# Router, slot gates and the way out of a branch in a two-block float32 kernel

## The chip, the cores and the metric

The kernel runs on one core of a Trainium2 chip. The metric is the device time of one execution in microseconds (us), the median of three runs; lower is better. Each run is compared with the kernel before on the same chip.

## The reference

The input is one sequence of 256 tokens of width 1024 in float32. A first block of two attention layers (dilated windows, grouped queries, attention to a memory) is followed by a second block of two layers. The change lies in the second block, whose layer is, in short:

```python
h = x @ w_in[l]                       # 1892 columns: queries, keys, values, latents
mix = [window_attention(h), sparse_attention_top64(h), latent_attention(h)]
x = layer_norm(ALPHA * x + concat(mix) @ w_out[l], ln1_g[l], ln1_b[l])
scores = sigmoid(x @ w_router)        # 16 experts in 4 groups
group  = argmax(sum of the two best biased scores in each group)
gates  = the two best experts of the group, normalised
y = sum_e gates[e] * (silu(x @ w_gate[l, e]) * (x @ w_up[l, e])) @ w_down[l, e]
x = layer_norm(ALPHA * x + y, ln2_g[l], ln2_b[l])
```

## The kernel before

The 256 tokens are two tiles of 128 rows. Every engine has its own program, written out by hand, and they meet at semaphores. `wait_ge` waits for a point of another engine, `then_inc(*x.did(...))` marks one, and `follow()` makes an engine wait for its own last instruction.

Each float32 weight goes through a ring in memory (filled by SP's DMA queue) and is cut in quarters of at most 128 x 1024: ACT writes the high part (`wH`, line 441), DVE the rest (`wL`, line 449). Five quarters fit (`NQ`). TensorE then makes three single-pass matmuls for one product (`mm3`, lines 508 to 510), and the last of a quarter gives the quarter's place back (`w_used`). A float32 matmul that isn't split appears as two matmul records, a transposition as one.

Stages of a layer `l` of the second block, in order:

- **h{l}0 to h{l}3**, the projections by `w_in`. The first is made tile by tile in `pe_proj_by_tiles`: tile 0, and after its sixth of eight steps the function `second_tile`, which turns tile 1 (8 transpositions, line 1661) and makes the "shift product" (line 1745: eight float32 matmuls of the layer norm's bias with the router's weights, 16 columns each). ACT copies that product (line 1854) and then goes on cutting weights.
- **attention**, in units. `dve_run` lets DVE choose the 64 best keys of a row in rounds of eight (`best`, lines 1991 and 1992) between the softmaxes of the units. Each unit ends with its output Y (line 894 or 1712), which TensorE turns (line 976).
- **p{l}**, the output projection, and layer norm 1: sums (1625), mean (1626), middle (1632), squares on ACT (1652), root by ACT (712, 713) and DVE (718 to 722), the scaled row (1643). Each tile has its own root.
- **router**: TensorE turns each tile's `middle` (1661), runs four multiplications by zero (`pe_idle`, line 517), and multiplies with the router's weights (1829). DVE makes logits (2072), scores and the chosen group (2075 to 2090); TensorE counts ranks (1837); DVE copies them (2095), takes the largest count (2096, 2097) and the slots (2098, 2101).
- **a branch** on the largest count. Here all engines take `few`: tokens are gathered by matmuls (2307), slot gates are made (2314) after the first expert's gate and up product, 16 experts run, and the result goes back (2356).
- **layer norm 2** (`act_finish`, `dve_finish`), still inside the branch; for layer 0 it ends with the turned tile 0 for h10 (`act_flip_exit`, `dve_flip_exit`). Tile 1 is turned after the branch.

The multiplications by zero give nothing to the result. They are placed where TensorE would wait.

Of the kernel before, what the change touches and what calls it, by code (L numbers as in the profile page):

```python
# [125 lines left out]
def program(nc, t, out, cols, keep):  # L126
# [76 lines left out]
    zeroR = sb("zeroR", P, 1, dt=F32R)  # L203
    blank = sb("blank", P, 1)
# [180 lines left out]
    first_normed, first_turned, second_normed = sem("first_normed"), sem("first_turned"), sem("second_normed")  # L385
# [15 lines left out]
    def write(pe, act, dve, pool, sp, branch):  # L401
# [1207 lines left out]
        for l in range(2):  # L1609
            for n, (a, b) in enumerate(SPLITS):  # L1610
                to_heads(f"h{l}{n}", hT, lambda kk, i, l=l: (first_turned, kk // 4 + 1) if l and not i else at("xT", l, i, kk - kk % 4), lambda i, a=a, b=b: H2[:, i, a:b])
# [27 lines left out]
        def dve_scaled(i, key):  # L1639
            r = small(1, "r", "ln", i, *key)  # L1640
            dve.wait_ge(at("scale", "ln", i, *key))
            for c, x in enumerate(in_two(X[:, i, :])):
                mm = dve.e.scalar_tensor_tensor(x, in_two(middle[i])[c], r[:, 0:1], lnw[:, 1, c * 512:(c + 1) * 512], MUL, ADD)
                if key[-1] == 0:
                    mm.then_inc((first_normed, second_normed)[i], 1)
                else:
                    mm.then_inc(*dve.did("x", *key, i, c))

        def act_add_and_norm(i, key):
            ss = small(1, "ss", i, *key)  # L1650
            act.wait_ge(at("mean", i, *key))
            act.e.activation(squares[:, :], X[:, i, :], SQUARE, bias=small(1, "mean", i, *key), accum_out=ss).then_inc(*act.did("sum", "ln", i, *key))
            act_root(("ln", i, *key), ss, 1, 1.0 / D, "eps5")

        def pe_flip_x(i, name, src, ready):
            for c, j0 in enumerate((0, 4)):
                b = att_bank(("xT", name, i, j0), (first_turned, c + 1) if name == "exit" else at("xT", name, i, j0))
# [20 lines left out]
        def act_flip_exit(way):  # L1678
            for j0 in (0, 4):
                act.wait_ge(at("turned", "xT", "exit", 0, j0))  # L1680
                act.e.activation(hT[0][:, j0:j0 + 4, 0:P], bank_of["xT", "exit", 0, j0].t[:, :].rearrange("p (j n) -> p j n", j=4),
                                 COPY).then_inc(*act.did("high", "exit", way, j0))

        def dve_flip_exit(way):
            for j0 in (0, 4):
                dve.wait_ge(at("high", "exit", way, j0))
                dve.e.tensor_tensor(hT[1][:, j0:j0 + 4, 0:P], bank_of["xT", "exit", 0, j0].t[:, :].rearrange("p (j n) -> p j n", j=4),
                                    hT[0][:, j0:j0 + 4, 0:P].bitcast(F32), SUB).then_inc(first_turned, 1)
# [45 lines left out]
        def pe_mix_layer(l):  # L1734
# [5 lines left out]
            def second_tile():  # L1740
                pe_flip_x(1, l, X, second)
# [5 lines left out]

            turn["proj"] = 2
            pe_proj_by_tiles(f"h{l}0", second_tile)
# [83 lines left out]
            ge = small(8, "ge", l)  # L1833
            pe.wait_ge(at("groups", l), (d_late, 32))
            for m, v, a, n, first in (("before", ge, 0, 8, True), ("ones", ge[:, 0:4], 4, 4, False),
                                      ("ones", ge[:, 0:4], 8, 4, True), ("ones", ge[:, 4:8], 8, 4, False)):
                mm = pe.e.matmul(b.t[:, a:a + n], K(m), v, start=first, stop=not first)
# [100 lines left out]
        def dve_mix_layer(l):  # L1938
            dve_cut(start(f"h{l}0") + 4)
            dve_flip_x(1, l)  # L1940
# [4 lines left out]
            dve.follow().tensor_copy(maskC[:, :, :], K("mC", 2)).then_inc(*dve.did("maskC", l))  # L1945
            dve_to(f"h{l}0")
# [80 lines left out]
            def behind_scores(n):  # L2027
# [5 lines left out]
                if 0 < n < 5:  # L2033
                    best(1, 2)
# [3 lines left out]
            def between(n):  # L2038
# [14 lines left out]
            for i in range(2):  # L2053
                dve_row_scale(i, (f"p{l}",))
# [10 lines left out]
        def dve_route(l):  # L2065
# [4 lines left out]
            for i in range(2):  # L2070
                dve.wait_ge(at("router", l, i))
                dve.follow().scalar_tensor_tensor(n32[0][:, 16 * i:16 * i + 16], banks[i].t[:, 0:16], small(1, "r", "ln", i, f"p{l}")[:, 0:1],
# [17 lines left out]
            dve.follow().tensor_tensor(ge3, ge3, bc(gk.unsqueeze(2), [P, 2, 4]), ALU.is_equal).then_inc(*dve.did("groups", l))  # L2090
# [7 lines left out]
            dve.follow().tensor_tensor(rank[:, 0:8], rank[:, 0:8], go, ADD).then_inc(*dve.did())  # L2098
# [5 lines left out]
        def dve_gates(l, way):  # L2104
# [4 lines left out]
            ge, go = [small(8, n, l).rearrange("p (t g) -> p t g", t=2).unsqueeze(3) for n in ("ge", "go")]  # L2109
# [141 lines left out]
        def act_finish(l, way):  # L2251
# [7 lines left out]
            for i in range(2):  # L2259
                act_add_and_norm(i, way)  # L2260
                if i == 0:
                    act_flip_exit(way)

        def dve_finish(l, way, ready, sums_in=(None, None)):
# [12 lines left out]
            for i in range(2):  # L2277
# [4 lines left out]
                if i == 0:  # L2282
                    dve_flip_exit(way)
# [10 lines left out]
        def pe_few(l):  # L2294
# [14 lines left out]
            def slot_gates():  # L2309
                b = att_bank((*way, "gates"), at(*way, "slot_gate"))  # L2310
# [84 lines left out]
            if l == 0:  # L2395
                pe_idle(10, att_bank((*way, "idle"), None))
# [197 lines left out]
```

## Time and profile before

| | us |
|---|---|
| median of three runs | 1122.07 (1122.01 to 1122.79) |
| profiled execution, its own time | 1123.5 |
| span of its instructions | 1122.2 |
| TensorE busy | 1075.3 |
| DVE busy | 886.3 |
| ACT busy | 743.1 |

The profile is one execution. The mean granted clock of TensorE over the span is 0.98. The chain that ended last is 50% TensorE, 31% DVE, 11% ACT and 5% issue. Layer 0 of the second block begins at about 541 us, its branch at about 669; layer 1 begins at 826 and its branch at 959. In a timeline row the columns are start, length, engine and line, operation, and in brackets the idle time before it with what ended it. In a row of the chain they are start, length and line.

### The profile page before, as it was taken

To read this page: it belongs to the slowest core of one execution; us is meant where nothing else is said; L and a number is where in the kernel's file an instruction comes from. 1 tells how busy PE (TensorE), PEld (TensorE's weight loads), DVE (VectorE), ACT (ScalarE), POOL (GpSimd) and SP (SyncE) were. 2 spreads that over 40 slices of the span, in tenths; PEclk is the share of its full clock that TensorE was granted. 3 is DMA by queue.
4 is the path that set the end of the run, shared out by engine and by line. 5 is a ranking of instruction groups with operands and counts; after the bars stand their busy time and mean duration, and the time that the engine had idled before them with its cause. 6 is when DMAs were issued, how large, how long until landed. Compare 5 with 4: busy or idle time off the path is not lost.

```text
span 1122.2 us, 14604 instructions
## 1 busy us (share of the span) xinstructions
PE 1075.3 (96%) x5486; PEld 923.2 (82%) x5486; DVE 886.3 (79%) x1473; ACT 743.1 (66%) x1318; POOL 0.2 (0%) x4
## 2 busy tenths in 40 slices
PE   9999999999998999999999999999989999999996
PEld 6788888888887888888987888888878878788885
DVE  5757757878678868767688779999977877899996
ACT  6656576566565766586464557998846555699993
POOL 0000000000000000000000000000000000000000
PEclk9999999999999999999997999999989989999998
DMA  9844444444434554726532427999845332599991
GB/s 349 328 170 150 151 169 169 150 150 151 151 113 134 204 188 160 227 75 204 169 116 76 150 76 242 364 374 374 318 129 192 110 115 75 165 352 363 385 379 44
DMA packets 131282, 223.34 MB, mean 199 GB/s; under 512 B 6016, under 2 KB 76416, under 8 KB 130944
## 3 DMA queue, kind: packets, MB, share of 16 engines
q1 hardware_dynamic: 127600, 215.40, 55.5%
q10 hardware_dynamic: 3600, 6.89, 2.0%
q8 instruction: 46, 0.75, 0.3%
q14 instruction: 36, 0.29, 0.1%
HBM read 221.23 MB, written 1.05 MB: 198 GB/s over the span
## 4 chain that ended last, share of the span: by engine, by line
PE 50%; DVE 31%; ACT 11%; issue 5%; DMA 1%; SPq 0%; ACTq 0%; DVEq 0%
DVE wL L449 14%; PE bank L508 12%; PE bank L509 11%; PE bank L510 11%; ACT wH L441 4%; PE bank L887 3%; PE bank L823 3%; PE bank L872 2%; DVE sm L764 1%; DVE qkv L767 1%; ACT S L846 1%; PE bank L2307 1%; DMA mem_rows<-in_mem 1%; DVE ys L2474 1%; DVE T L2490 1%
## 5 line engine op out<-in xcount | busy, mean ns | idle before, releaser
L449 DVE TENSOR_TENSOR wL<-ring,wH 128x1024 fp32r<-128x1024 f32 (+1 forms) x316 | 375.2, 1212 | 120.2 <-ACT wH L441 119.4
L441 ACT ACTIVATE wH<-ring 128x1024 fp32r<-128x1024 f32 (+1 forms) x316 | 319.8, 1045 | 25.9 <-PE bank L510 15.9
L508 PE MATMUL bank<-wH,hTH 128*128 128x512 f32 (+2 forms) x592 | 230.4, 389 | 5.1 <-DVE wL L449 4.0
L509 PE MATMUL bank<-wL,hTH 128*128 128x512 f32 (+2 forms) x592 | 223.8, 378 | 0.0
L510 PE MATMUL bank<-wH,hTL 128*128 128x512 f32 (+2 forms) x592 | 223.6, 378 | 0.0
L508 PEld LDWEIGHTS bank<-wH,hTH 128*128 128x128 f32 x592 | 113.1, 191 | 22.9 <-DVE wL L449 8.4
L510 PEld LDWEIGHTS bank<-wH,hTL 128*128 128x128 f32 x592 | 113.0, 191 | 14.1
L509 PEld LDWEIGHTS bank<-wL,hTH 128*128 128x128 f32 x592 | 113.1, 191 | 13.0 <-issue 0.5
L508 PE MATMUL bank<-wH,xgH 128*128 128x512 f32 x256 | 102.8, 402 | 2.5 <-DVE wL L449 2.3
L509 PE MATMUL bank<-wL,xgH 128*128 128x512 f32 x256 | 98.1, 383 | 0.0
L510 PE MATMUL bank<-wH,xgL 128*128 128x512 f32 x256 | 98.1, 383 | 0.0
L846 ACT ACTIVATE S<-bank,sm 128x256 f32<-128x256 f32 (+1 forms) x144 | 59.7, 429 | 41.6 <-DVE sm L838 41.6
L508 PEld LDWEIGHTS bank<-wH,xgH 128*128 128x128 f32 x256 | 49.3, 193 | 14.7 <-DVE wL L449 7.5
L878 ACT ACTIVATE PT<-bank 128x512 f32<-128x512 f32 x56 | 31.2, 597 | 44.1 <-PE bank L872 44.1
L510 PEld LDWEIGHTS bank<-wH,xgL 128*128 128x128 f32 x256 | 49.1, 192 | 7.0
L509 PEld LDWEIGHTS bank<-wL,xgH 128*128 128x128 f32 x256 | 49.4, 193 | 5.3
L576 ACT ACTIVATE qkv<-bank,factors 128x512 f32<-128x512 f32 x50 | 33.0, 688 | 26.2 <-PE bank L510 26.2
L449 DVE TENSOR_TENSOR wL<-ring_G,wH 128x1024 fp32r<-128x1024 f32 x40 | 48.4, 1218 | 1.1 <-ACT wH L441 1.0
L508 PE MATMUL bank<-wH,gh 128*128 128x512 f32 x128 | 49.0, 383 | 0.0
L449 DVE TENSOR_TENSOR wL<-ring_K,wH 128x1024 fp32r<-128x1024 f32 x40 | 48.3, 1219 | 0.8 <-ACT wH L441 0.7
L510 PE MATMUL bank<-wH,gh 128*128 128x512 f32 x128 | 48.6, 379 | 0.0
L509 PE MATMUL bank<-wL,gh 128*128 128x512 f32 x128 | 48.5, 379 | 0.0
(294 smaller groups left out, 1861.3 us busy)
## 6 DMA issues: line engine op xcount, KB each, us to landing
ring<-in_w_in_a SPq DMA_DIRECT2D x44, 1024.0 KB, 5.1
ring<-in_w_out SPq DMA_DIRECT2D x20, 1024.0 KB, 4.9
ring<-in_w_down SPq DMA_DIRECT2D x20, 1024.0 KB, 7.0
ring<-in_w_gate SPq DMA_DIRECT2D x36, 512.0 KB, 5.6
ring<-in_w_up SPq DMA_DIRECT2D x36, 512.0 KB, 7.2
ring<-in_w_in_b SPq DMA_DIRECT2D x14, 1024.0 KB, 5.2
ring<-in_w_in SPq DMA_DIRECT2D x8, 1024.0 KB, 5.3
ring<-in_w_mem_kv SPq DMA_DIRECT2D x7, 1024.0 KB, 6.5
```

The source lines that it names most:

```text
L441: act.e.activation(quarter_parts(q)[0], quarter_in_ring(q), COPY).then_inc(w_high, 1)
L449: dve.e.tensor_tensor(lo, quarter_in_ring(q), hi.bitcast(F32), SUB).then_inc(w_low, 1)
L508: pe.e.matmul(o, a[0], high, start=first, stop=False)
L509: pe.e.matmul(o, a[0], low, start=False, stop=False)
L510: return pe.e.matmul(o, a[1], high, start=False, stop=last)
L576: act.e.activation(two_halves(dst(i)), from_woven(bank_of["proj", name, i].t, slab_w[name]), COPY, scale=factor(key)[:, i:i + 1] if key el ...
L764: dve.follow().tensor_reduce(ss.rearrange("p (t h) -> p t h", t=2), sq.rearrange("p t (h d) -> p t h d", d=P), AX, ADD).then_inc(*dve.did( ...
L823: mm = pe.e.matmul(score_bank(u, s // each)[:, s % each, :], u.qh(s)[:, i * P:(i + 1) * P], u.kh(s)[:, k:k + n], start=u.mask is None, sto ...
L846: act.e.activation(u.S[:, s, 0:n], score_bank(u, s // each)[:, s % each, :], EXP, bias=nb[:, s:s + 1], scale=u.scale, accum_out=u.den[:, s ...
L872: tr = pe.e.transpose(b.t[:, s * P:(s + 1) * P], u.S[:, s, kt * P:(kt + 1) * P], ident)
L878: act.e.activation(u.PT[:, kt, :, :].rearrange("p h q -> p (h q)"), bank_of["turn", u.name, kt].t[:, :], COPY).then_inc(*act.did("PT", u.n ...
L887: mm = pe.e.matmul(b.t[:, s * u.dv:(s + 1) * u.dv], u.PT[:, kt, s, :], u.vh(s, kt), start=kt + s == 0, stop=kt == u.nk - 1, skip_group_che ...
```

## The change

It does nine things:

1. The shift product leaves `second_tile` and moves to the router, behind the transpositions of tile 0, in the place of four multiplications by zero; ACT's copy moves with it.
2. Layer norm 1 takes the roots of both tiles together, after tile 1's squares.
3. The chosen groups are written as fp32r, with fp32r copies of the two counting matrices, and the ranks are single-pass matmuls. The copies are made once, in layer 0 (two 128 x 128 on DVE).
4. The copy of the ranks (2095) goes; its readers read the bank.
5. In the unit with number 2, one of two rounds of `best` for tile 1 moves behind the output of the unit before it and the turned outputs' low part.
6. Three multiplications by zero precede the slot gates.
7. For layer 1, tile 1 is turned by ACT and DVE inside the branch of layer 0, as is the cut of h10's last quarter, which now comes ahead of tile 0's part on ACT and DVE.
8. For layer 1, TensorE turns tile 1 after all eight steps of tile 0 (not six), followed by four multiplications by zero.
9. The multiplications by zero at the end of layer 0's branch become 13 (from 10).

```diff
-        def pe_proj_by_tiles(name, meanwhile):
+        def pe_proj_by_tiles(name, meanwhile, behind):
...
-                    if i == 0 and kk == 6:
+                    if 8 * i + kk == behind:
                         meanwhile()
...
         def act_add_and_norm(i, key):
-            ss = small(1, "ss", i, *key)
+            both = key[0][0] == "p"
+            ss = small(2, "ss", *key)[:, i:i + 1] if both else small(1, "ss", i, *key)
             act.wait_ge(at("mean", i, *key))
...
+            if not both:
+                act_root(("ln", i, *key), ss, 1, 1.0 / D, "eps5")
+            elif i:
+                act_root(("ln", *key), small(2, "ss", *key), 2, 1.0 / D, "eps5")
...
-            def second_tile():
-                pe_flip_x(1, l, X, second)
+            def shift_product():
...
+            def second_tile():
+                pe_flip_x(1, l, X, second)
+                if l:
+                    pe_idle(4, att_bank(("idle", l, 0), None))
...
-            pe_proj_by_tiles(f"h{l}0", second_tile)
+            pe_proj_by_tiles(f"h{l}0", second_tile, 8 if l else 6)
...
-                pe_idle(4, banks[2 + i])
+                if i == 0:
+                    shift_product()
+                else:
+                    pe_idle(4, banks[2 + i])
...
-            act_cut(start(f"h{l}0") + 4)
-            act_flip_x(1, l)
-            act.wait_ge(at("shift product", l))
-            act.e.activation(small(16, "shift", l), bank_of["shift", l].t[:, 0:16], COPY).then_inc(*act.did("shift", l))
+            if l == 0:
+                act_cut(start(f"h{l}0") + 4)
+                act_flip_x(1, l)
...
+                if i == 0:
+                    act.wait_ge(at("shift product", l))
+                    act.e.activation(small(16, "shift", l), bank_of["shift", l].t[:, 0:16], COPY).then_inc(*act.did("shift", l))
...
+            if l == 0:
+                for n, name in enumerate(("before", "ones")):
+                    dve.e.tensor_copy(countR[:, n, :], K(name)).then_inc(*dve.did("counting"))
...
                 if 0 < n < 5:
-                    best(1, 2)
+                    best(1, 1 if n == 2 else 2)
...
+                if n == 5:
+                    best(1, 1)
...
-            dve.follow().tensor_copy(rank, bank_of["rank", l].t[:, 0:12]).then_inc(*dve.did("rank", l))
-            dve.follow().tensor_reduce(most, rank[:, 8:12], AX, MAX).then_inc(*dve.did())
+            dve.follow().tensor_reduce(most, bank_of["rank", l].t[:, 8:12], AX, MAX).then_inc(*dve.did())
...
                 dve_row_scale(i, way)
                 dve_scaled(i, way)
                 if i == 0:
-                    dve_flip_exit(way)
+                    dve_cut(start("h10") + 4)
+                dve_flip_exit(i, way)
...
             def slot_gates():
+                pe_idle(3, att_bank((*way, "idle", 1), None))
...
-                pe_idle(10, att_bank((*way, "idle"), None))
+                pe_idle(13, att_bank((*way, "idle"), None))
```

## Rows read from the trace of the kernel before

**Rows 1.** Stretches of core 0: us; busy PE, PEld, DVE, ACT, POOL; granted clock; DMA.

```profile
545.00:550.00 5.00, 5.00 (x39) 5.00 (x38) 3.24 (x5) 2.34 (x5) 0.00 (x0) 1.00 0.66 210
...
655.00:660.00 5.00, 5.00 (x37) 4.66 (x37) 4.68 (x12) 4.43 (x10) 0.00 (x0) 1.00 0.00 0
...
834.80:841.60 6.80, 6.22 (x18) 6.05 (x19) 4.34 (x7) 2.11 (x4) 0.00 (x0) 0.50 0.78 246
602.80:616.20 13.40, 13.20 (x38) 9.74 (x37) 9.59 (x26) 6.03 (x22) 0.00 (x0) 0.50 0.00 1
684.70:687.90 3.20, 3.20 (x10) 2.65 (x11) 3.06 (x6) 1.05 (x2) 0.00 (x0) 0.50 0.43 104
```

**Rows 2.** The chain that ended last, beginning of layer 0.

```profile
545.83 1.69 PE bank L1745 x16
```

**Rows 3.** The chain, router of layer 0.

```profile
656.49 0.87 PE bank L1661 x8
657.36 0.88 PE bank L517 x4
658.24 1.69 PE bank L1829 x16
...
666.86 1.33 DVE X L1643 x2
...
668.28 0.18 DVE sm L2095
```

**Rows 4.** Timeline, router of layer 0.

```profile
657.93 1.15 ACT L1652 ACTIVATE squares<-X,sm 128x1024 f32<-128x1024 f32 x1
...
663.45 0.23 DVE L2072 SCALAR_TENSOR_TENSOR sm<-bank,sm 128x16 f32<-128x16 f32 x1 [0.66 <-PE bank L1829]
```

**Rows 5.** Timeline of unit 2: DVE, layer 0 and then layer 1.

```profile
624.73 0.42 DVE L894 TENSOR_TENSOR Y<-bank,sm 128x256 f32<-128x256 f32 x1 [1.48 <-PE bank L887]
...
627.64 0.69 DVE L834 TENSOR_REDUCE mx<-bank 128x2 f32<-128x512 f32 x1 [0.39 <-PE bank L823]
...
638.81 0.42 DVE L894 TENSOR_TENSOR Y<-bank,sm 128x256 f32<-128x256 f32 x1
...
915.40 0.69 DVE L834 TENSOR_REDUCE mx<-bank 128x2 f32<-128x512 f32 x1 [1.15 <-PE bank L823]
```

**Rows 6.** The chain, unit 2 of layer 1.

```profile
909.21 0.44 DVE top L1991
...
910.19 0.44 DVE top L1991
...
912.24 0.66 PE bank L976 x4
```

**Rows 7.** Timeline of TensorE, slot gates of layer 0.

```profile
683.07 2.21 PE L2314 MATMUL bank<-SG,OH 128*128 128x4 f32 x16 [0.52 <-DVE SG L2123]
```

**Rows 8.** Who waited for whom, 680 to 712 us: total, times, longest.

```profile
DVE wL L449 <- ACT wH L441: 0.5, 1, 0.5
DVE gh L2463 <- ACT gh L2412: 0.2, 1, 0.2
```

**Rows 9.** Timeline, way out of layer 0's branch and beginning of layer 1.

```profile
824.37 1.32 PE L1661 MATMUL bank<-const,X 128*128 128x128 f32 x8 [1.20 <-DVE X L1643]
...
825.69 1.35 DVE L1687 TENSOR_TENSOR hTL<-bank,hTH 128x512 fp32r<-128x512 f32 x2 [0.72 <-ACT hTH L1681]
...
831.76 1.32 PE L1661 MATMUL bank<-const,X 128*128 128x128 f32 x8 [1.83 <-DVE X L1643]
...
832.96 0.90 ACT L441 ACTIVATE wH<-ring 128x832 fp32r<-128x832 f32 x1 [2.62 <-issue]
...
837.00 0.96 ACT L441 ACTIVATE wH<-ring 128x904 fp32r<-128x904 f32 x1 [2.01 <-issue]
...
844.01 0.52 ACT L576 ACTIVATE arena<-bank 128x416 f32<-128x416 f32 x1 [0.69 <-PE bank L510]
```

**Rows 10.** The chain, layer 0, where the granted clock is 0.50.

```profile
611.63 1.04 PE bank L872 x4
```

More of the change, by code:

```diff
@@ L1610, in write @@
             for n, (a, b) in enumerate(SPLITS):
-                to_heads(f"h{l}{n}", hT, lambda kk, i, l=l: (first_turned, kk // 4 + 1) if l and not i else at("xT", l, i, kk - kk % 4), lambda i, a=a, b=b: H2[:, i, a:b])
+                to_heads(f"h{l}{n}", hT, lambda kk, i, l=l: ((first_turned, second_turned)[i], kk // 4 + 1) if l else at("xT", l, i, kk - kk % 4), lambda i, a=a, b=b: H2[:, i, a:b])
         def heads(buf, a, n):
@@ L1639, in dve_scaled @@
         def dve_scaled(i, key):
-            r = small(1, "r", "ln", i, *key)
-            dve.wait_ge(at("scale", "ln", i, *key))
+            both = key[0][0] == "p"
+            r = small(2, "r", "ln", *key)[:, i:i + 1] if both else small(1, "r", "ln", i, *key)
+            dve.wait_ge(at("scale", "ln", *key) if both else at("scale", "ln", i, *key))
             for c, x in enumerate(in_two(X[:, i, :])):
@@ L1649, in act_add_and_norm @@
         def act_add_and_norm(i, key):
-            ss = small(1, "ss", i, *key)
+            both = key[0][0] == "p"
+            ss = small(2, "ss", *key)[:, i:i + 1] if both else small(1, "ss", i, *key)
             act.wait_ge(at("mean", i, *key))
-            act.e.activation(squares[:, :], X[:, i, :], SQUARE, bias=small(1, "mean", i, *key), accum_out=ss).then_inc(*act.did("sum", "ln", i, *key))
-            act_root(("ln", i, *key), ss, 1, 1.0 / D, "eps5")
+            act.follow().activation(squares[:, :], X[:, i, :], SQUARE, bias=small(1, "mean", i, *key), accum_out=ss).then_inc(
+                *(act.did("sum", "ln", *key) if both else act.did("sum", "ln", i, *key)))
+            if not both:
+                act_root(("ln", i, *key), ss, 1, 1.0 / D, "eps5")
+            elif i:
+                act_root(("ln", *key), small(2, "ss", *key), 2, 1.0 / D, "eps5")
+        exit_name = ("exit", 1)
         def pe_flip_x(i, name, src, ready):
             for c, j0 in enumerate((0, 4)):
-                b = att_bank(("xT", name, i, j0), (first_turned, c + 1) if name == "exit" else at("xT", name, i, j0))
+                b = att_bank(("xT", name, i, j0), ((first_turned, second_turned)[i], c + 1) if name in exit_name else at("xT", name, i, j0))
                 pe.wait_ge(ready[c])
@@ L1832, in pe_mix_layer @@
             b = att_bank(("rank", l), at("rank", l))
[L1833 to L1837, printed above, removed]
+            ge = geR[:, :]
+            pe.wait_ge(at("groups", l), at("counting"))
+            for m, v, a, n, first in ((0, ge, 0, 8, True), (1, ge[:, 0:4], 4, 4, False),
+                                      (1, ge[:, 0:4], 8, 4, True), (1, ge[:, 4:8], 8, 4, False)):
+                mm = pe.e.matmul(b.t[:, a:a + n], countR[:, m, :], v, start=first, stop=not first)
             mm.then_inc(*pe.did("ranks", l))
@@ L1938, in dve_mix_layer @@
         def dve_mix_layer(l):
-            dve_cut(start(f"h{l}0") + 4)
-            dve_flip_x(1, l)
+            if l == 0:
+                dve_cut(start(f"h{l}0") + 4)
+                dve_flip_x(1, l)
             dve_upto(f"h{l}1")
@@ L2052, in dve_mix_layer @@
                 dve_middle(i, (f"p{l}",), ln_loaded(l, 1))
-            for i in range(2):
-                dve_row_scale(i, (f"p{l}",))
+            dve.wait_ge(at("sum", "ln", f"p{l}"))
+            dve_root(("ln", f"p{l}"), small(2, "ss", f"p{l}"), 2, 1.0 / D, "eps5")
             dve_scaled(0, (f"p{l}",))
@@ L2071, in dve_route @@
                 dve.wait_ge(at("router", l, i))
-                dve.follow().scalar_tensor_tensor(n32[0][:, 16 * i:16 * i + 16], banks[i].t[:, 0:16], small(1, "r", "ln", i, f"p{l}")[:, 0:1],
+                dve.follow().scalar_tensor_tensor(n32[0][:, 16 * i:16 * i + 16], banks[i].t[:, 0:16], small(2, "r", "ln", f"p{l}")[:, i:i + 1],
                                                   small(16, "shift", l), MUL, ADD).then_inc(*dve.did("logits", l, i))
@@ L2089, in dve_route @@
             dve.follow().tensor_reduce(gk, ge3, AX, MAX).then_inc(*dve.did())
-            dve.follow().tensor_tensor(ge3, ge3, bc(gk.unsqueeze(2), [P, 2, 4]), ALU.is_equal).then_inc(*dve.did("groups", l))
+            dve.wait_ge(at("ranks", 0) if l else None)
+            dve.follow().tensor_tensor(geR[:, :].rearrange("p (t g) -> p t g", t=2), ge3, bc(gk.unsqueeze(2), [P, 2, 4]), ALU.is_equal).then_inc(*dve.did("groups", l))
+            ge = geR[:, :].bitcast(F32)
             go, rank, most = small(8, "go", l), small(12, "rank", l), small(1, "most", l)
@@ L2094, in dve_route @@
             dve.wait_ge(at("ranks", l))
-            dve.follow().tensor_copy(rank, bank_of["rank", l].t[:, 0:12]).then_inc(*dve.did("rank", l))
-            dve.follow().tensor_reduce(most, rank[:, 8:12], AX, MAX).then_inc(*dve.did())
+            dve.follow().tensor_reduce(most, bank_of["rank", l].t[:, 8:12], AX, MAX).then_inc(*dve.did())
             dve.follow().tensor_copy(count[:, :], most[0:1, :]).then_inc(*dve.did("count", l))
-            dve.follow().tensor_tensor(rank[:, 0:8], rank[:, 0:8], go, ADD).then_inc(*dve.did())
+            dve.follow().tensor_tensor(rank[:, 0:8], bank_of["rank", l].t[:, 0:8], go, ADD).then_inc(*dve.did("rank", l))
             dve.wait_ge(dve.last())
@@ L2108, in dve_gates @@
             b4 = n32[1].rearrange("p (t g e) -> p t g e", t=2, g=4)
-            ge, go = [small(8, n, l).rearrange("p (t g) -> p t g", t=2).unsqueeze(3) for n in ("ge", "go")]
+            ge, go = [a.rearrange("p (t g) -> p t g", t=2).unsqueeze(3) for a in (geR[:, :].bitcast(F32), small(8, "go", l))]
             dve.follow().tensor_tensor(b4, b4, bc(ge, [P, 2, 4, 4]), MUL).then_inc(*dve.did())
@@ L2261, in act_finish @@
                 if i == 0:
-                    act_flip_exit(way)
+                    act_cut(start("h10") + 4)
+                act_flip_exit(i, way)
         def dve_finish(l, way, ready, sums_in=(None, None)):
```

20 lines of the change are left out of this document (11 added, 9 removed).

## The prediction

> **What bounds the kernel now.** I read the page's chain first. It is half TensorE and a third DVE, so no engine bounds the whole, and each edit has to be priced where it stands. I then read the chain and the timeline of each place that the diff touches, and last the granted clock over them. The reader is to see three things. At the beginning of layer 0 and in the router the chain is TensorE's [rows 2, 3], so work taken from it or given to it there counts in full. Unit 2 of layer 1 is DVE's [rows 6]. And behind the way out of layer 0's branch the clock is lost: in 834.8 to 841.6 it is 0.50, and the 18 matmuls that keep TensorE busy for 6.2 us there [rows 1] would take half that at full clock.
>
> **The change, part by part.** The sum is made against the profiled execution's 1123.5 (its span of 1122.2 and 1.3 around it). That execution lies 1.4 above the median of the runs, 1122.07, and I take what the sum gives from the median as well.
>
> *Shift product out of h00.* Its 16 records take 1.69 on the chain [rows 2], between matmuls of TensorE on both sides, and what ACT and DVE cut next waits for places that TensorE gives back, so it comes forward too. **-1.69.** The two fp32r copies of 128 x 128 are unseen; the nearest rows, a small copy of 0.18 [rows 3] and a cut of 0.90 for 128 x 832 [rows 9], bound one at 0.2 and 0.9. They are hidden beside the matmuls of h00, where DVE is busy 3.24 us of 5.00 [rows 1]; uncovered they would cost 0.4 to 1.8. I take 0.
>
> *Shift product into the router.* It costs 1.69 there as well and replaces four multiplications by zero of 0.88 [rows 3], so TensorE is 0.81 later at the second tile's router product, and DVE's logits wait for just that [rows 4]. **+0.81 in each layer, +1.62.** ACT is now held for the product's copy until 659.1, so tile 1's squares, which began at 657.93 [rows 4], begin at 659.3. With 1.35 of squares, 0.5 of root on ACT, 0.6 on DVE and 1.4 of scaled row DVE is ready for the logits at 663.2. TensorE's product, so far at 663.45 less a few hundredths, now ends at 664.25: the later root is hidden by 1.0, and the second root that DVE saves is worth nothing, because DVE waits there already (0.66 [rows 4]). Without that cover the root is what is late next.
>
> *Ranks.* The matmuls run beside the scaled row of 1.33 that ends at 668.19 [rows 3]; they are hidden with two passes, so one pass gives nothing. The copy of 0.18 [rows 3] and 0.02 behind it are on the chain. **-0.20 in each layer, -0.40**; if the reduction is slower from the bank, it is by less than the whole copy, so the bounds are -0.40 and 0.
>
> *The moved round.* A round of `best` is 0.98 from start to start [rows 6]. In layer 1 it stands ahead of the output for which TensorE waits, and behind that DVE has 1.15 idle [rows 5]: **-0.98.** In layer 0 DVE waits 1.48 for TensorE at that output, so nothing comes earlier; the round now stands ahead of the next maximum, before which only 0.39 was idle, and makes it 0.6 late. DVE catches up nowhere until 638.81, where it was just in time [rows 5]: **+0.50** (0 if TensorE is later by then).
>
> *Slot gates.* TensorE is idle 0.52 ahead of them [rows 7]. Three multiplications (0.22 each, from four in 0.88 [rows 3]) fill that and delay the gates by 0.1. Behind the gates the clock is 0.50 up to 688 [rows 1]: some 3 us of matmuls, seven of them, that need 1.5 at full clock. If the filling holds the clock, 1.2 is free on TensorE less 0.1. But DVE is nearly full from there on; its waits up to 712 are 0.5, 0.2 and another 0.2 [rows 8], so it can't come forward by more than 0.9. Between 0 and 0.9 I take the middle: **-0.50 in each layer, -1.00.**
>
> *Way out.* DVE has a cut of 1.03 ahead of tile 0's low part, where 0.72 was idle [rows 9], so h10 starts 0.3 later, and the later steps with it. TensorE now runs all eight steps of tile 0, to 831.0. Tile 1's transpositions (1.32 with the wait between them [rows 9]) start at 832.1, its low part is there at 834.1, the four multiplications end at 834.3, and with 24 matmuls of 0.175 h10 ends at 838.5 if the clock holds. So far it ended at 844.0 [rows 9]. That is 5.5 us for TensorE. But ACT's exit from the branch is 2.62 of "issue" ahead of 832.96 [rows 9]; it lay beside the wait for tile 1's row, and now begins behind tile 1's copies, at 834.0. ACT comes out at 836.6, issues four DMAs (2.01 [rows 9]), and cuts three quarters (0.96 each) before it copies h10's outputs. The second copy, so far at 844.01 [rows 9], comes at 842.0, and the projections' norm hangs on it. So what is late next is ACT's exit, and TensorE waits 2 us for h11's first quarter. **-2.05**; the bounds are 0 (that wait costs the clock again) and -5 (the exit is covered after all). On SP's queue the load that waits for h10's last cut comes 9 us earlier; it can meet only ACT's four small transfers, which are needed 15 us later. The three more multiplications at the end of the branch, 0.66, lie in 1.20 of idle [rows 9]: 0.
>
> Sum: -1.69 + 1.62 - 0.40 - 0.98 + 0.50 - 1.00 - 2.05 = **-4.0**: 1119.5 for the profiled execution, 1118.1 for the median.
>
> **What speaks against the change.** In the router before, transpositions (0.87), four multiplications (0.88) and 16 small records (1.69) [rows 3] alternate, and the clock stays at 1.00 [rows 1]. Behind the change come transpositions, 32 small records and transpositions, 5.2 us without one 512-column matmul. The nearest row that held is h00's: 0.87 of transpositions and 1.69 of shift product, at 1.00 [rows 1, 2]. The nearest that fell is h10's: a wait of 1.83, transpositions and shift product, and then 0.50 [rows 1, 9]. The new stretch lies between the two, and I hold it likelier than not that both routers keep the clock or lose little.
>
> The Trainium skill says in "TensorE: Matmul & The Clock Gate", Part 4 (PE-mode transpose), that transpositions don't count as TensorE being busy in the way matmuls do. By that rule the clock falls in both routers, and the time is that of the second rival below; by the row of h00, where transpositions stood in the stretch and the clock held, it is 1118.1.
>
> **The rivals.**
>
> *The clock falls in one router* (0.27), late. Four transpositions take 1.04 at 0.50 [rows 10], where eight take 0.92 at full clock: 1.2 lost on the second tile's, and 0.8 on its four multiplications. Together 2.0: 1120.1.
>
> *It falls in both, and is still down in the twelve multiplications behind* (0.17). This is the case on the other side. The twelve take 5.2 instead of 2.6, and the ranks wait behind them on TensorE; 0.6 is to spare before the groups are chosen, so 2.0 more. A layer loses 4.0, the two 8.0: 1126.1. It makes the kernel slower from 3.1 a layer on. Against it: the clock at 1.00 in both routers now, with less than half of the stretch in multiplications.
>
> *The way out gives nothing* (0.13), because ACT's exit grows or TensorE's wait for h11 brings the clock down. For it: nothing in the trace shows what the exit overlaps. Without its term the sum is -1.95: 1120.1. That the change does nothing there, while the rest does what it says, is this case.
>
> *The long slow stretch of the attention shrinks* (0.08). The clock is 0.50 from 602.8 to 616.2 [rows 1]. What comes before moves by 1.7 us, so what TensorE does when the clock is decided is something else. Losing a fourth to a half of these 13.4 us saves 1.7 to 3.4: 1114.7 to 1116.4. It could begin earlier as well, which I leave to the range.
>
> **How the numbers follow.** The sum as it stands has 0.35, and with its own bounds is 1116 to 1119.5; it is the likeliest, so 1118.1 is the prediction. A measurement of this kernel tells 0.2% (2.24) from nothing, so faster is below 1119.8. That is the forecast (0.35), the attention's case (0.08) and 0.17 of the 0.40 of the two cases at 1120.1, whose spread reaches over that line: 0.60. The rest of these, 0.23, and 0.04 of the case of both routers are the same: 0.27. Slower is 0.13. The range of 1114.5 to 1122.5 takes in all but the case of both routers and little else.
>
> **What would show it.** Right: clock 1.00 from 684 to 688 and over h10; the shift product between L1661 and L1829 with DVE's L2072 still waiting for L1829; no L2095; ACT's idle "issue" behind tile 1's copies, and TensorE waiting for DVE's cut at h11. Wrong: a clock of 0.50 between the transpositions and the ranks in either layer; an exit longer than 2.6; a slot gate stage that ends earlier with the experts ending at the same distance behind it.

## The result and the profile after

The changed kernel takes 1115.68 us (median of seven, 1111.98 to 1117.88); the kernel before, on the same chip, 1122.79. The ratio is 0.9933, 95% interval 0.9917 to 0.9948: 7.1 us less, where I had forecast 4.0. The time lies in the range I gave (1114.5 to 1122.5). The profiled execution spans 1114.3 us, against 1122.2, at a mean granted clock of 0.989, against 0.980.

The total says little about the steps. So I cut both traces at the same instructions, from one to the next along the kernel, and compared the lengths (us, worked out from the start times of TensorE's first record at each place):

| from ... to ... | before | after | difference | my terms |
|---|---|---|---|---|
| start to h00's first transposition | 539.45 | 540.32 | +0.87 | none |
| to the turned latents of layer 0 | 21.05 | 19.45 | -1.60 | -1.69 |
| to the first turned output | 42.72 | 42.72 | 0 | 0 |
| to the router | 53.11 | 50.61 | -2.50 | +0.50 |
| to the gathers | 13.47 | 14.18 | +0.71 | +0.61 |
| to the slot gates | 13.27 | 13.27 | 0 | 0 |
| to the last matmul of the way back | 137.53 | 135.99 | -1.54 | -0.50 |
| out of the branch, to the turned latents of layer 1 | 30.91 | 31.23 | +0.32 | -2.05 |
| to the first turned output | 42.71 | 42.72 | 0 | 0 |
| to the router | 52.22 | 49.05 | -3.17 | -0.98 |
| to the gathers | 13.47 | 14.19 | +0.72 | +0.61 |
| to the slot gates | 13.28 | 13.27 | 0 | 0 |
| to the last matmul of the way back | 137.63 | 135.95 | -1.68 | -0.50 |
| to the end | 11.35 | 11.39 | 0 | 0 |

What I priced with rows of the chain (h00, the router with its ranks) came out to a tenth of a us. The clock's places did not: the attention of both layers and the slot gates gave 7.4 us more than forecast, and the way out gave nothing. (The 0.87 at the start goes with a stretch at half clock that is 6.8 us long instead of 3.4, far ahead of the change.) Of the -2.50 in layer 0's attention, 0.9 isn't the change's doing. The trace of before had the long stretch of [rows 1] there; b_slot (below), whose attention is unchanged, didn't have it and took 52.17.

Stretches of the changed kernel, with the columns of [rows 1]:

```profile
602.80:616.20 13.40, 13.40 (x79) 11.04 (x76) 11.15 (x30) 6.85 (x23) 0.00 (x0) 1.00 0.01 2
635.10:638.40 3.30, 3.30 (x14) 1.84 (x13) 1.38 (x3) 0.60 (x1) 0.00 (x0) 0.50 0.00 0
680.70:687.90 7.20, 7.20 (x42) 6.34 (x43) 7.06 (x10) 4.78 (x7) 0.00 (x0) 1.00 0.72 224
822.80:829.60 6.80, 6.15 (x20) 5.66 (x21) 4.72 (x13) 2.93 (x6) 0.00 (x0) 0.50 0.50 157
907.00:914.00 7.00, 6.57 (x32) 4.92 (x32) 6.04 (x16) 4.39 (x12) 0.00 (x0) 1.00 0.64 190
654.00:661.00 7.00, 7.00 (x63) 6.89 (x61) 4.30 (x12) 3.83 (x9) 0.00 (x0) 1.00 0.00 0
```

Beside [rows 1]: the attention's 13.4 us at 0.50 are at 1.00, with 79 matmuls where there were 38, and so is what follows the slot gates. The router keeps 1.00 with the shift product in it. But the way out is at 0.50 again, only earlier (822.8 where it was 834.8), and 635.1 to 638.4 is new.

The chain in the router of layer 0, after (as [rows 3]), then DVE's and TensorE's timeline there and at the slot gates (as [rows 4, 7]):

```profile
653.26 0.87 PE bank L1670 x8
654.14 1.69 PE bank L1753 x16
655.83 1.79 PE bank L1845 x16
657.62 0.92 PE bank L1670 x8
658.54 0.87 PE bank L518 x4
659.41 1.71 PE bank L1845 x16
```

```profile
661.14 0.23 DVE L2096 SCALAR_TENSOR_TENSOR sm<-bank,sm 128x16 f32<-128x16 f32 x1 [0.82 <-PE bank L1845]
...
665.96 0.16 DVE L2121 TENSOR_REDUCE sm<-bank 128x1 f32<-128x4 f32 x1
...
679.86 0.82 PE L518 MATMUL bank<-zeroR,identR 128*128 128x512 f32 x3
680.55 1.95 PE L2342 MATMUL bank<-SG,OH 128*128 128x4 f32 x16
```

The product costs its 1.69 in the place of 0.88, DVE still waits for the second tile's logits (0.82, as [rows 4]), and the reduction from the bank is no longer than a copy. The way out, timeline of all engines, as [rows 9]:

```profile
816.75 3.00 PE L518 MATMUL bank<-zeroR,identR 128*128 128x512 f32 x13
...
820.30 0.33 PE L1670 MATMUL bank<-const,X 128*128 128x128 f32 x1 [0.55 <-DVE X L1645]
...
822.74 1.75 PE L1670 MATMUL bank<-const,X 128*128 128x128 f32 x7 [2.11 <-issue]
...
823.68 0.60 ACT L1690 ACTIVATE hTH<-bank 128x512 fp32r<-128x512 f32 x1 [4.01 <-PE bank L1670]
...
831.63 1.04 PE L1670 MATMUL bank<-const,X 128*128 128x128 f32 x8
...
835.39 0.34 ACTq L1127 DMA_DIRECT2D lnw<-in_ln_g  x1
...
837.32 2.65 ACT L442 ACTIVATE wH<-ring 128x904 fp32r<-128x904 f32 x3 [3.96 <-PE bank L511]
...
839.46 0.46 PE L509 MATMUL bank<-wH,hTH 128*128 128x452 f32 x1 [1.33 <-DVE wL L450]
...
839.87 0.91 ACT L577 ACTIVATE arena<-bank 128x416 f32<-128x416 f32 x2
```

TensorE turns one of eight blocks and then stands for 2.11 us of "issue". Nothing that the profile shows is missing to it, and behind it the clock is 0.50. In [rows 9] the same eight are one group of 1.32. The DMA view of 820 to 822 us has one transfer on TensorE's instruction queue (q8), 16 KB from 820.57 on:

```profile
q8 instruction: 1, 0.02, 3.0%
```

### The profile page after: what moved, and what is told of

Same layout as the page of the kernel before. It is cut to its first block, busy times and chain, and to the rows that moved or that the text cites. A ratio compares the mean times of both kernels' runs of the same rounds, so it can differ in the third digit from the quotient of the medians.

```text
span 1114.3 us, 14586 instructions
## 1 busy us (share of the span) xinstructions
PE 1066.6 (96%) x5483; PEld 914.4 (82%) x5483; DVE 883.8 (79%) x1465; ACT 742.3 (67%) x1314; POOL 0.2 (0%) x4
## 4 chain that ended last, share of the span: by engine, by line
PE 47%; DVE 33%; ACT 12%; issue 6%; DMA 1%; SPq 0%; ACTq 0%; DVEq 0%
DVE wL L450 14%; PE bank L509 12%; PE bank L511 11%; PE bank L510 11%; ACT wH L442 4%; PE bank L888 3%; PE bank L824 2%; ACT S L847 2%; DVE sm L765 1%; DVE mx L835 1%; DVE qkv L768 1%; PE bank L2334 1%; DVE qkv L2014 1%; PE bank L873 1%; DMA mem_rows<-in_mem 1%
## 5 line engine op out<-in xcount | busy, mean ns | idle before, releaser
L577 ACT ACTIVATE qkv<-bank,factors 128x512 f32<-128x512 f32 x50 | 33.0, 688 | 26.2 <-PE bank L511 26.1
```

Of the source, the lines that this page charges most:

```text
L577: act.e.activation(two_halves(dst(i)), from_woven(bank_of["proj", name, i].t, slab_w[name]), COPY, scale=factor(key)[:, i:i + 1] if key el ...
```

## The experiments

Executions of one kernel spread over 3.6 us (q_shiftback) to 11.8 us (noexit) here, and the mean clock of each goes with its time. So beside the median I give the mean time at half clock of a kernel's executions, worked out as twice (1 - mean clock) times the span, averaged. Within a kernel, one us of it costs 0.32 us of time (a line through all 186 executions, each kernel's mean taken out).

| kernel | median us | executions | ratio to before | at half clock, us |
|---|---|---|---|---|
| before (beside the rest) | 1122.13 to 1122.64 | 70 | | 39.7 |
| after | 1115.68 | 7 | 0.9933 | 26.1 |
| pad32 | 1113.59 | 6 | 0.9926 (0.9903 to 0.9948) | 24.9 |
| pad64 | 1118.43 | 12 | 0.9958 (0.9937 to 0.9979) | 33.3 |
| pad96 | 1111.67 | 6 | 0.9911 (0.9890 to 0.9932) | 20.4 |
| pad96_again | 1114.93 | 6 | 0.9930 (0.9906 to 0.9954) | 25.2 |
| noexit | 1118.11 | 12 | 0.9956 (0.9938 to 0.9974) | 33.9 |
| q_noexit | 1116.29 | 12 | 0.9950 (0.9931 to 0.9969) | 28.4 |
| q_shiftback | 1112.24 | 6 | 0.9926 (0.9904 to 0.9947) | 19.3 |
| q_best2 | 1119.04 | 12 | 0.9977 (0.9961 to 0.9994) | 38.4 |
| q_noslot | 1118.61 | 12 | 0.9974 (0.9959 to 0.9989) | 33.7 |
| b_best | 1118.15 | 12 | 0.9976 (0.9959 to 0.9993) | 32.1 |
| b_slot | 1117.64 | 7 | 0.9956 (0.9939 to 0.9973) | 30.9 |
| fill | 1112.24 | 6 | 0.9910 (0.9890 to 0.9931) | 20.4 |

### Where TensorE's code lies: pad32, pad64, pad96

```diff
             down(15)
+            if l == 0:
+                pe_idle(32, att_bank((*way, "idle"), None))
```

This stands at the end of `pe_all`, the branch that isn't taken; pad64 and pad96 have 64 and 96 in the place of 32. The kernels called q_ and fill, further down, are padded in the same place, by 85 to 99, so that the code behind the branch lies about where it lies in pad96.

> The changed kernel, with 32 multiplications by zero added at the end of the other branch of layer 0, which is not taken. Nothing that runs is different; only the place of TensorE's code behind the branch moves, by 64 weight loads and matmuls. Theory 'code place': the 2.11 us of issue at 820.63 is a wait for an instruction fetch just behind the jump (the 16 KB fetch on queue 8 begins at 820.57), and it depends on where that code lies; here the stall moves or goes. If it goes, h10 starts 2.1 us earlier, the clock may hold, and the time falls by 2 to 4 us against the changed kernel (ratio to before near 0.990 instead of 0.9933). Rival 'exit itself': the stall belongs to leaving the branch with more work behind it, and stays at 2.1 us behind the first transposition, time unchanged within 0.5 us.

> As with 32, with 64 multiplications by zero in the branch that is not taken (128 instructions). 'Code place': the stall's place against the transpositions differs from that with 0 and with 32; where it falls into a wait it costs nothing, as before the change. 'Exit itself': the same 2.1 us at the same transposition.

> As with 32 and 64, with 96 (192 instructions). 'Code place': of the three at most one has a stall of over 1 us between the transpositions of tile 0, and the best of them is 2 to 4 us faster than the changed kernel. 'Exit itself': all three alike and equal to the changed kernel.

Timeline of pad96 at the same place, and a stretch of it:

```profile
818.99 1.32 PE L1670 MATMUL bank<-const,X 128*128 128x128 f32 x8 [0.55 <-DVE X L1645]
...
834.77 0.90 ACT L577 ACTIVATE arena<-bank 128x416 f32<-128x416 f32 x2
```

```profile
818.90:835.00 16.10, 12.96 (x71) 11.30 (x72) 11.72 (x24) 6.91 (x12) 0.00 (x0) 1.00 0.43 135
```

The eight are one group of 1.32 again, and the clock is 1.00 all the way. From the last matmul of the way back to the turned latents pad96 takes 27.45 us, pad32 27.47, pad64 28.22 and the changed kernel 31.23. Only code that doesn't run was added, so the stall was one of code place: it was there in both kernels without padding that have the 13 multiplications (2.11 here, 1.38 in noexit, whose line follows), and in none of the nine traces of padded ones.

```profile
822.37 1.03 PE L1670 MATMUL bank<-const,X 128*128 128x128 f32 x7 [1.38 <-issue]
```

The Trainium skill, "Runtime: NRT & Kernel Launch", Instruction fetch mechanics, says that code is fetched in blocks of 16 KiB in sequence, and that a taken branch whose target isn't at hand stalls until it has been fetched; the trace agrees in part, with 2.11 us and a 16 KB fetch that begins at the same time. But such a fetch begins 3.1 to 4.0 us behind the last matmul of the way back in all 14 traces, and only two of them stall. The one here takes 0.96 us and ends at 821.53, 1.2 before TensorE goes on. That the place of the code decides is shown; that TensorE waits for this fetch is argued.

The medians don't repeat that gain so clearly: the 30 padded executions lie at 1114.9 in the mean, the seven of the changed kernel at 1115.1. pad64 shows one reason. No stage of its trace is more than 0.8 us longer than pad96's up to 886 us, and then the clock falls in the attention of layer 1:

```profile
886.30:899.90 13.60, 13.59 (x38) 10.17 (x39) 9.64 (x27) 5.78 (x22) 0.00 (x0) 0.50 0.00 0
```

That attention is 55.60 us long in pad64 and 49.09 in pad96. Whether this is chance stays open: pad64's twelve executions lie at 1117.4 in the mean and the twelve of pad96 at 1113.1, further apart than their spread makes likely, and no run tells whether the place of the code has a hand in it.

### The way out: noexit, q_noexit

```diff
-                if i == 0:
-                    act_cut(start("h10") + 4)
-                act_flip_exit(i, way)
+                if i == 0:
+                    act_flip_exit(i, way)
...
-            pe_proj_by_tiles(f"h{l}0", second_tile, 8 if l else 6)
+            pe_proj_by_tiles(f"h{l}0", second_tile, 6)
```

DVE likewise; tile 1's part and the cut go back behind the branch, and the four multiplications go. noexit is this from the changed kernel, q_noexit from pad96.

> The changed kernel with the way out as it was before (tile 1 turned and h10's last quarter cut behind the branch, after six steps of tile 0, no four multiplications by zero); the shift product stays in the router, the 13 multiplications at the branch's end stay. If my term for the way out was right in kind (-2.05) and the stall of 2.11 us ate it, this kernel is as fast as the changed one within 1 us, more if the clock behind the exit is 0.50 for as long. If the way out is worth something even with the stall, it is 1 to 2 us slower. Rival: the way out costs time, and this kernel is 1 us or more faster.

> The changed kernel padded by 96 multiplications in the untaken branch (where TensorE had no stall behind tile 0's first transposition and the clock stayed at 1.00), but with the way out as before the change: tile 1 is turned and h10's last quarter cut behind the branch. Theory 'right in kind': without the stall the way out is worth the 2.05 us of my term, so h10's outputs come about 2 us later than in the padded kernel, and the clock falls to 0.50 over h10 as it did before. Rival 'worth nothing': the stage from the last matmul of the experts to h11 is as long here, within 0.5 us.

In q_noexit the stage is 30.20 us (22.70 to h10's second output and 7.50 behind it), with the clock at 0.50 from 829.8 to 836.6; in pad96 27.45. So the way out is worth 2.75 in these traces, and 3.0 by the medians (1116.29 against the 1113.3 of the twelve executions of pad96). "Right in kind" holds, and by the stages the stall took more than all of it.

The 2.75 is one pair of traces. The five traces with the old way out, all with some half clock in it, have 28.93 (noexit), 30.20, and 29.72, 29.81 and 30.91 (b_best, b_slot, before), where six of the eight padded ones with the new one have 27.43 to 27.60. The last three also have the shift product in h10, which is worth 0.56 (q_shiftback, below). Less that, the worth is 1.3 to 2.9 us, and much of that range is how long the clock was down. noexit itself gave no clear answer. Its median is 2.4 above the changed kernel's (1118.11 against 1115.68), more than its expectation had for a way out that pays. Yet its stage is 2.3 shorter (28.93 against 31.23), and its trace loses its time in the attentions instead: 52.41 and 55.42 us, against 50.61 and 49.05.

### The shift product back: q_shiftback

```diff
             def second_tile():
                 pe_flip_x(1, l, X, second)
+                shift_product()
...
-                if i == 0:
-                    shift_product()
-                else:
-                    pe_idle(4, banks[2 + i])
+                pe_idle(4, banks[2 + i])
```

ACT's copy goes back too.

> The padded kernel (92, for the same code place) with the shift product back behind tile 1's transpositions in both layers, and the four multiplications by zero back in the router. By my terms: 1.69 more in h00, 0.81 less in each router: +0.1 us in sum, with L1's shift product at the beginning of h10 another +1.7. Theory 'phase': the attention's long stretch at clock 0.50 is not set by any one edit; its share of executions stays as in the changed kernel. Rival 'the shift product's place moved it': with 1.7 us back in h00 the stretch near 602 to 616 returns in the profile, and the mean time at half clock rises by some 10 us.

h00 is 21.05 us again, to the hundredth of the kernel before. The router is 13.26: 0.92 shorter than with the product, and 0.21 shorter than before the change, which is the ranks' part. In h10 the product, with 3.4 us at half clock beside it, costs 0.56 (20.51 against 19.95 to the second output). The time is that of pad96 within their spread, with the least time at half clock of all, so the product's place is not what moves the clock in the attention. In the router this trace has 3.4 us at 0.50 too, from 665.6 on, and the way from the gathers to the slot gates takes 14.48 us instead of 13.27.

### The moved round: q_best2, b_best

```diff
-                    best(1, 1 if n == 2 else 2)
+                    best(1, 2)
...
-                if n == 5:
-                    best(1, 1)
```

q_best2 undoes it in pad96; b_best makes it alone in the kernel before.

> The padded kernel with both rounds of best for tile 1 ahead of unit 2's neighbour, as before the change. My terms: 0.98 us later in layer 1 at the output for which TensorE waits, 0.5 us earlier in layer 0: +0.5 us in sum. Rival 'clock': the longer wait of TensorE there is what brought the clock to 0.50 from 913.3 to 920.1, so that this stretch returns and costs 2 us more: +2.5 us.

> The kernel before, with one edit of the change: one of unit 2's two rounds of best for tile 1 moves behind the output and the turned outputs' low part. My terms: -0.98 in layer 1 and +0.50 in layer 0, so -0.5 us. Theory 'clock through the wait': removing TensorE's wait in that unit keeps the clock at 1.00 from 913 to 920 in layer 1, so the mean time at half clock falls by about 7 us and the time by 2 to 4 us in all. If undoing the round in the changed kernel cost 7.4 us for this reason alone, this kernel gains 5 us or more; if part of that was the spread of the executions or hangs on the other edits, less.

Two kernels that differ from the one before in a single edit show it best. b_slot (below) has the round where it was; its timeline of TensorE, where it waits for DVE's outputs of unit 2 and of the unit S0 behind it, in layer 0, then unit 2 in layer 1, and two stretches:

```profile
620.40 0.66 PE L976 MATMUL bank<-const,Y 128*128 128x128 f32 x4 [1.23 <-DVE Y L894]
...
637.63 0.63 PE L976 MATMUL bank<-const,Y 128*128 128x128 f32 x4 [0.61 <-DVE Y L894]
...
907.86 0.91 PE L976 MATMUL bank<-const,Y 128*128 128x128 f32 x4 [1.23 <-DVE Y L894]
```

```profile
621.40:628.20 6.80, 6.80 (x18) 5.09 (x18) 4.48 (x15) 2.18 (x9) 0.00 (x0) 0.50 1.01 330
908.20:918.30 10.10, 10.10 (x27) 7.43 (x26) 5.80 (x17) 4.05 (x12) 0.00 (x0) 0.50 0.90 311
```

The same of b_best, with the round moved:

```profile
619.64 0.66 PE L976 MATMUL bank<-const,Y 128*128 128x128 f32 x4 [0.24 <-DVE Y L894]
...
634.74 1.09 PE L976 MATMUL bank<-const,Y 128*128 128x128 f32 x4 [1.29 <-DVE Y L894]
...
907.01 0.65 PE L976 MATMUL bank<-const,Y 128*128 128x128 f32 x4 [0.24 <-DVE Y L894]
```

```profile
634.70:638.00 3.30, 3.26 (x12) 2.46 (x14) 1.72 (x2) 0.60 (x1) 0.00 (x0) 0.50 0.01 4
908.00:918.00 10.00, 10.00 (x60) 8.36 (x61) 9.05 (x26) 5.75 (x18) 0.00 (x0) 1.00 0.92 311
```

The reader is to see that a wait was moved and hardly shortened: 1.23 becomes 0.24 at unit 2, and 0.61 becomes 1.29 at S0. Behind a wait of 1.23 at unit 2 the clock fell all five times that a trace has one. Behind a wait of 1.3 at S0 it fell 13 times of 20, so there the wait alone doesn't decide. Behind waits of 0.24 or 0.61 it never fell. At unit 2 long products are still to come (60 matmuls in 10 us at full clock, 27 in as many at half), at S0 there is short work. In the traces of before, b_slot and q_best2 the clock falls behind unit 2 in five of six layers, and behind S0 in none. Of the eleven traces with the moved round none has a stretch that begins behind unit 2; nine have the one of layer 0 behind S0, four the one of layer 1 (fill, below, has the wait at S0 filled and neither). Undone, the edit costs 5.8 us (1119.04 against 1113.3); alone it gains 4.1 by the medians (1118.15 against 1122.21) and 2.7 by the ratio. All are more than any sum of work; "clock through the wait" holds, in size and in place, with the lower of the two gains that b_best's expectation named.

### The slot gates: q_noslot, b_slot

```diff
             def slot_gates():
-                pe_idle(3, att_bank((*way, "idle", 1), None))
```

q_noslot takes the three out of the padded kernel; b_slot puts them into the one before.

> The padded kernel (99, for the same code place) without the three multiplications by zero ahead of the slot gates. My term: the clock falls to 0.50 for 3.4 us behind the gates in both layers, which costs 0.5 us in each, 1.0 in sum; the traces of before and after suggest 1.0 in each, 2.0 in sum. Rival: the clock holds without them too, and nothing changes but 0.1.

> The kernel before, with only the three multiplications by zero ahead of the slot gates. My term: -1.0 us; by the traces of before and after -2.0. Theory 'two stretches': the clock is 1.00 behind the gates in both layers, the mean time at half clock falls by 6.8 us. Rival 'spread': the 6.9 us that taking them out of the padded kernel cost was mostly attention stretches that happened to fall there, and this kernel gains no more than 2 us.

From the gates to the end of the branch's matmuls, q_noslot takes 137.52 in both layers and b_slot 135.98 in both: 1.54 a layer; before the change it was 137.53 and 137.63, after it 135.99 and 135.95. DVE's timeline of b_slot, at the instructions of [rows 8]:

```profile
687.98 0.42 DVE L2464 TENSOR_TENSOR gh<-bank,gh 128x256 fp32r<-128x256 f32 x1
688.32 1.22 DVE L449 TENSOR_TENSOR wL<-ring,wH 128x1024 fp32r<-128x1024 f32 x1
...
690.58 0.41 DVE L2490 TENSOR_TENSOR T<-T,bank 128x256 f32<-128x256 f32 x1
```

The same instructions before, with two of their waits:

```profile
691.00 1.23 DVE L449 TENSOR_TENSOR wL<-ring,wH 128x1024 fp32r<-128x1024 f32 x1 [0.52 <-ACT wH L441]
...
693.55 0.42 DVE L2489 TENSOR_TENSOR T<-T,bank 128x256 f32<-128x256 f32 x1 [0.19 <-ACT T L2438]
```

The two waits of [rows 8] and the 0.19 here are gone, 0.95 in sum. The rest is that an instruction that has not waited starts some 0.1 before the shown end of the one ahead of it (688.32 + 1.22 ends at 689.54, and the next cut starts at 689.45), and one that has waited doesn't. The first cut after a wait comes 0.61 earlier for a wait of 0.52, and at the cut behind the third wait 1.32 of the 1.54 are there; the other 0.2 stays open.

That it is the clock, and not the multiplications as such, b_best shows. It has none ahead of its slot gates, and TensorE waits 0.54 there in layer 1, but this once the clock holds behind them:

```profile
970.20:973.60 3.40, 3.40 (x19) 2.84 (x19) 3.26 (x6) 1.13 (x2) 0.00 (x0) 1.00 0.69 180
```

The way to the end of the branch's matmuls is then 135.98 us, and 137.55 in its layer 0, where the clock fell. Without the multiplications the clock fell behind the gates in five of six layers, with them in none of 22. Undone, the edit costs 5.3 us and alone it gains 4.6, against 3.1 to 3.2 by the stages; the rest is within the spread of the executions.

### Filling more waits: fill, pad96_again

```diff
+                if n == 4:
+                    pe_idle(2, att_bank(("idle", l, 4), None))
...
+            pe_idle(2, att_bank(("idle", l, 5), None))
             outputs(6, 2, 0)
...
+                    pe_idle(2, att_bank(("idle", l, 6), None))
                     flip_one(("kS", l), ...
...
+                if n == 9:
+                    pe_idle(5, att_bank(("idle", l, 7), None))
                 if n in OUT_AT:
```

> A version meant to beat both: the changed kernel, padded in the untaken branch for the same code place as with 96, and with eleven multiplications by zero in each layer's attention, where TensorE waits: two ahead of the last values of the latent units, two ahead of the first turned outputs, two ahead of the keys of the sparse units, five ahead of the turned outputs at step 9 (where TensorE is idle 1.29 us before the clock falls at 633.4). If the stretches near 601, 618, 635 and 922 follow TensorE's idle time there, they go, and the time falls by 1.5 to 3 us against the padded kernel, with a narrower spread. Rival: the multiplications delay what comes behind them by 0.2 each where they outlast the wait, or move the banks' order so that a bank is waited for, and the time is the same or 1 to 2 us longer.

> The padded kernel once more, beside the others, to see how far two samples of the same kernel lie apart: within 1.5 us of 1111.7 if six executions settle a median, further if the clock's chance in the attention decides it. Its trace also tells whether a stretch at half clock that is missing in one execution is there in another.

In fill no stretch is left in either attention: layer 0's is 49.01 us, where pad96 has 50.68, at a price of 0.55 in each layer ahead of the first output (43.28 instead of 42.73). But this execution lost the clock in the router, 19.01 us to the gathers instead of 14.18. pad32 lost it there too:

```profile
654.20:667.80 13.60, 13.60 (x50) 12.24 (x50) 6.32 (x23) 3.83 (x9) 0.00 (x0) 0.50 0.00 1
```

```profile
657.30:667.50 10.20, 10.20 (x34) 8.76 (x34) 5.78 (x20) 2.31 (x5) 0.00 (x0) 0.50 0.00 1
```

With 1112.24 fill is the equal of pad96 at best; that it beats the changed kernel (by 0.3%) isn't settled by six executions. pad96_again is the same program as pad96, and its profile has what the other lacks, a stretch in layer 0's attention at the very place of [rows 1]:

```profile
600.00:613.60 13.60, 13.29 (x38) 9.90 (x38) 9.66 (x27) 6.04 (x22) 0.00 (x0) 0.50 0.01 2
```

It makes that attention 55.48 us long instead of 50.68, and the medians of the two samples lie 3.3 us apart. So whether the long stretch near 600 comes is settled anew in each execution. Whether an edit makes it rarer or more frequent, these runs don't show.

## Why the prediction was right, and where it was not

*Shift product out of h00*: right, -1.60 for -1.69, and 21.05 again in q_shiftback. The fp32r copies cost nothing, as said.

*Shift product into the router*: right in kind; 0.92 a layer for 0.81. The common root is hidden, DVE waits 0.82 for the product.

*Ranks*: right, -0.21 a layer for -0.20.

*The moved round*: the step that failed first. "-0.98 in layer 1" was right at unit 2 (the way to it is 17.03 instead of 18.00 us in b_best's and b_slot's layer 0) but most of it is given back one unit later: from unit 2's output to S0's, without a stretch between them, 14.17 in the kernel before and 15.09 after. I read the 1.15 of idle behind the round in [rows 5] as cover and didn't look at the next output. The 14.17 comes from a unit 2 that was 4 us late, and where it is as late with the round moved the way takes 14.85 to 14.88; no trace has the old order at full clock all the way. So 0.7 to 0.9 of the 0.98 goes back, and in work the edit is worth 0.3 us a layer at most, by this estimate. My term for layer 0 (+0.50) rested on the 1.48 that DVE waited in [rows 5], in a unit that the stretch of 602.8 to 616.2 had made late; at full clock TensorE waits 1.23 there (b_slot), as in layer 1. What the round is worth is clock: the 6.8 us at 0.50 from 913.3 are gone, and 3.17 us with them in that stage.

*Slot gates*: right in kind, mis-sized. I capped the term at 0.9 and took 0.5; it is 1.54 and 1.68, 3.2 in sum. The cap failed because waits of 0.95 cost 1.3 to 1.5 once what stands behind each of them is counted.

*Way out*: the likeliest course was right in kind, and was not what ran. ACT's exit is what comes last (its DMAs are issued 2.04 after tile 1's copies end, and TensorE waits 1.33 for h11's quarter, where I said 2). Without the stall the stage is 3.5 shorter than in the trace of before (2.3 shorter than in b_best's and b_slot's, which leave it as it was). Of that the way out itself is 2.75 by the one pair and the product that left h10 0.56. With it the changed kernel loses 0.32. My rival "the way out gives nothing" had the right size for another reason: I named ACT's exit and the wait for h11, and it was the place of TensorE's own code.

*The rivals of the clock*: it fell in neither router of the changed kernel's trace, but in 4 of the 20 router stages of the ten traces with the product there, at a cost of 1.65 to 4.8 us each. So "in one router" was a real case, more so than its 2.0 us. The four traces without the product have it in none of 8 before the gathers, too few to tell the two apart, and two of them (b_best, q_shiftback) lost 2.8 and 1.2 us just behind. The Trainium skill, "TensorE: Matmul & The Clock Gate", Part 4 (PE-mode transpose), has it that transpositions don't count as busy in the way matmuls do. That is no rule for each time here: the same instructions kept the clock 16 times. *The attention's long stretch* went, as the rival at 0.08 had it, but it is in three of those ten traces at layer 0 and in two at layer 1. So what I took for a case of the change differs between executions of one program, and that it was absent in the profiled one was luck.

The sum of 4.0 came near 7.1 by errors of both signs: of the 7.8 by which the spans differ, I had 2.4 too much for the way out, 2.2 too little for the slot gates and 5.2 too little in the two attentions; the start took 0.9 and the rest 0.3. By the means, the time fell by 7.0 (1122.1 to 1115.1), of which the 13.6 us less at half clock, at 0.32 each, are 4.3.

What stays open: why the medians show so little of the stall that padding removes, and why noexit is the slower kernel with the shorter stage. One trace of the changed kernel can't say in how many of its executions the stall occurs.

## What to carry to other kernels

Where the clock fell behind a wait of 1.2 or 1.3 us, the attention took 1.5 to 4.8 us longer; when an edit moves a wait, look for where it arrives and for what is queued behind it there. Price an edit from a stretch at full clock, since a row inside or behind a stretch at half clock shows who waits for whom the wrong way round. Compare stage by stage between the same instructions, and have two traces of the same program before a stretch at half clock is put down to an edit.

## What the runs showed of the hardware

- Code that never runs changed the time of code that does: 64 to 192 instructions in the untaken branch removed a stall of 2.11 us on TensorE behind the jump, and with it 6.8 us at half clock.
- The same program keeps the clock at 1.00 from 600 to 613.6 us in one execution and has 0.50 in the next (4.8 us longer), while the stage ahead of it is 42.71 to 42.74 us long in thirteen of fourteen traces (the other is fill's).
- Three multiplications by zero (0.82 us on TensorE, in a gap of 0.5) take 1.54 us off a stage of 137.5 by keeping the clock; where it held without them the stage was as short (135.98, b_best, layer 1).
- On DVE a wait costs about 0.1 us more than it lasts.
